# Inner norms of a two-layer diffusion step: two of eight chunks shifted and scaled by GpSimd

## The reference

```
def layer_norm(x, g, b):
    xf = x.astype(F32)
    xc = xf - xf.mean(-1, keepdims=True)
    var = (xc * xc).mean(-1, keepdims=True)
    return (xc * lax.rsqrt(var + EPS) * g + b).astype(x.dtype)

def modulate(x, shift, scale):
    return x * (1 + scale) + shift
...
for layer in range(DEPTH):
    hp = modulate(xp, mp[0], mp[1])            # the latent half (xs) likewise
    op = mixer(hp)
    xp = layer_norm(ALPHA * xp + mp[2] * op, ln_g[layer, 0], ln_b[layer, 0])
    hp = modulate(xp, mp[3], mp[4])
    fp = moe_ffn(hp, router_w, router_b, moe_wg[layer], moe_wu[layer], moe_wd[layer])
    xp = layer_norm(ALPHA * xp + mp[5] * fp, ln_g[layer, 1], ln_b[layer, 1])
```

## Time and profile before

| | |
|---|---|
| median of three runs | 1114.04 us (1110.41 to 1114.46) |
| the profiled execution's own time | 1112.55 us |
| its span in the trace | 1110.8 us |
| mean granted TensorE clock | 0.948 of full speed |
| busy: TensorE, VectorE, ScalarE, GpSimd | 983.9, 349.3, 217.0, 134.4 us |
| DMA | 299.5 MB, mean 270 GB/s |

### The profile page before, as it was taken

How to read it: one execution, slowest core, us unless ns; L and a number is a source line. 1 busy time by engine, 2 the same in 40 slices (tenths; PEclk the granted TensorE clock), 3 DMA queues, 4 the chain that set the end, 5 groups by cost and what they waited for, 6 DMA issues and landing times. The chain is left out here.

```text
span 1110.8 us, 13877 instructions
## 1 busy us (share of the span) xinstructions
PE 983.9 (89%) x5502; PEld 569.6 (51%) x5502; DVE 349.3 (31%) x820; ACT 217.0 (20%) x513; POOL 134.4 (12%) x149
## 2 busy tenths in 40 slices
PE   7899998897989898977999998899696989898986
PEld 3344466764323333336788677578585323333334
DVE  1101125248101010123333677668427400101004
ACT  2110045031200010013333421213102200000003
POOL 1000000000000000001000266575001000000000
PEclk9899999896989999998999899999896999999998
DMA  9995772162999999995655400222234699999981
GB/s 379 401 408 219 315 307 76 38 245 107 401 431 427 427 428 427 427 428 228 244 211 207 173 1 1 76 76 77 76 130 173 254 414 427 428 427 426 429 377 39
DMA packets 22444, 299.50 MB, mean 270 GB/s; under 512 B 2592, under 2 KB 2720, under 8 KB 4320
## 3 DMA queue, kind: packets, MB, share of 16 engines
q1 hardware_dynamic: 20880, 292.45, 64.3%
q0 software_dynamic: 1488, 6.03, 1.4%
HBM read 295.32 MB, written 3.15 MB: 269 GB/s over the span
## 5 line engine op out<-in xcount | busy, mean ns | idle before, releaser
L547 PE MATMUL bank<-ring,arena 128*32 128x512 f32 (+1 forms) x1216 | 203.0, 607 | 7.1 <-DMA ring<-slots 7.1
L565 PE MATMUL bank<-ring,arena 128*32 128x512 f32 (+1 forms) x608 | 112.4, 671 | 32.3 <-DMA ring<-slots 27.2
L547 PEld LDWEIGHTS bank<-ring,arena 128*32 128x32 f32 (+1 forms) x1216 | 61.2, 125 | 144.1 <-issue 133.6
L821 DVE TENSOR_TENSOR arena<-arena,bank 128x256 f32<-128x256 f32 x28 | 11.8, 421 | 302.1 <-ACT arena L650 302.1
L975 PE MATMUL bank<-act_t,ring 128*128 128x256 f32 x384 | 89.4, 387 | 6.3 <-DVE act_t L432 6.3
L1529 PE MATMUL bank<-ring,act_t 128*128 128x512 f32 x192 | 87.4, 608 | 3.2 <-DVE act_t L1794 2.5
L975 PEld LDWEIGHTS bank<-act_t,ring 128*128 128x128 f32 x384 | 72.4, 194 | 20.0 <-DVE act_t L432 6.7
L565 PEld LDWEIGHTS bank<-ring,arena 128*32 128x32 f32 (+1 forms) x608 | 32.1, 134 | 94.3 <-issue 84.5
L888 POOL COPY arena<-arena 128x512 f32 (+1 forms) x34 | 17.5, 515 | 391.8 <-PE bank L547 306.5
L1529 PEld LDWEIGHTS bank<-ring,act_t 128*128 128x128 f32 x192 | 36.3, 195 | 51.2 <-issue 46.4
L905 PE MATMUL bank<-act_t,ring 128*128 128x256 f32 x256 | 59.9, 396 | 1.6 <-ACT act_t L1267 0.9
(11 more groups left out here) (323 smaller groups left out, 1284.5 us busy)
## 6 DMA issues: line engine op xcount, KB each, us to landing
ring<-slots SPq DMA_DIRECT2D x138, 2048.0 KB, 12.7
cst<-consts SPq DMA_DIRECT2D x1, 1260.5 KB, 36.8
act_t<-x_t POOLq DMA_DIRECT2D x1, 1024.0 KB, 12.7
ring<-state POOLq DMA_DIRECT2D x1, 1024.0 KB, 5.2
out_st<-arena POOLq DMA_DIRECT2D x4, 256.0 KB, 2.8
out_y<-arena SPq DMA_DIRECT2D x4, 256.0 KB, 2.1
par<-params SPq DMA_DIRECT2D x1, 613.0 KB, 3.9
arena<-nat_bias POOLq DMA_DIRECT2D x1, 512.0 KB, 22.1
```

Of the source, the lines that this page charges most:

```text
L547: last = pe.matmul(bk[to:to + wide, :], x[:, 4 * m + c, wide * e:wide * e + wide], w[:, c, 512 * t:512 * t + 512], start=(m == 0 and c == ...
L565: last = pe.matmul(bank[3][to:to + wide, :], ht[:, col + wide * e:col + wide * e + wide], w[:, f, 512 * t:512 * t + 512], start=(f == 0), ...
```

## The change

In each inner norm chunks 7 and 3 go to GpSimd: for each chunk two instructions of 128 x 128 (one for each half of the tokens), a multiply and an add in one, with the two columns as scalars. It waits for the first L424 before chunk 7 and for the second before chunk 3, and raises `ln_h` once behind the fourth. ScalarE keeps chunks 4, 5 and 6, VectorE 0, 1 and 2. `ln_h` now counts three for a site, and the waits are changed to that, those of the last norm too.

```diff
--- before.py
+++ after.py
@@ -375,7 +375,7 @@
                 pe.wait_ge(S("ln_eps"), site + 1)
                 ada_rows(pe, jobs[k], bank[LN_JOB_BANKS[k]], jobs[0])
             if site < 3:
-                pe.wait_ge(S("ln_h"), 2 * site + 2)
+                pe.wait_ge(S("ln_h"), 3 * site + 3)
 
         def ln_act(act, ch, site):
             for h in range(4):
@@ -392,7 +392,7 @@
             if site < 3:
 
                 act.wait_ge(S("ln_norm"), 2 * site + 1)
-                for c in range(4, KC):
+                for c in range(4, 7):
                     for s in range(2):
                         i = site * 16 + 2 * c + s
                         last = act.activation(act_t[:, c, s * P:(s + 1) * P], res[:, c, s * P:(s + 1) * P], ACT.Identity,
@@ -426,18 +426,23 @@
             if site < 3:
 
                 dve.wait_ge(S("ln_norm"), 2 * site + 2)
-                rv = res[:, 0:4, :].rearrange("p c (s n) -> p (c s) n", s=2)
-                av = act_t[:, 0:4, :].rearrange("p c (s n) -> p (c s) n", s=2)
-                ch.link(dve.tensor_tensor(av, rv, bcast(mod_g[:, site * 16:site * 16 + 8], P), ALU.mult))
-                dve.tensor_tensor(av, av, bcast(mod_b[:, site * 16:site * 16 + 8], P), ALU.add).then_inc(S("ln_h"), 1)
+                rv = res[:, 0:3, :].rearrange("p c (s n) -> p (c s) n", s=2)
+                av = act_t[:, 0:3, :].rearrange("p c (s n) -> p (c s) n", s=2)
+                ch.link(dve.tensor_tensor(av, rv, bcast(mod_g[:, site * 16:site * 16 + 6], P), ALU.mult))
+                dve.tensor_tensor(av, av, bcast(mod_b[:, site * 16:site * 16 + 6], P), ALU.add).then_inc(S("ln_h"), 1)
             if site in LN_JOBS:
                 ada_store(dve, LN_JOBS[site][0], bank[LN_JOB_BANKS[0]])
 
         def ln_pool(pool, site):
 
-            pool.wait_ge(S("ln_norm"), 2 * site + 2)
-            if site < 3:
-                pool.wait_ge(S("ln_h"), 2 * site + 2)
+            for h, c in enumerate((7, 3)):
+                pool.wait_ge(S("ln_norm"), 2 * site + h + 1)
+                for s in range(2):
+                    i = site * 16 + 2 * c + s
+                    last = pool.tensor_scalar(act_t[:, c, s * P:(s + 1) * P], res[:, c, s * P:(s + 1) * P],
+                                              mod_g[:, i:i + 1], mod_b[:, i:i + 1], ALU.mult, ALU.add)
+            last.then_inc(S("ln_h"), 1)
+            pool.wait_ge(S("ln_h"), 3 * site + 3)
 
             for c in range(KC):
                 i = site * 16 + 2 * c
@@ -1666,7 +1671,7 @@
             for q in range(2):
                 for s in range(2):
                     for j in range(4):
-                        pe.wait_ge(S("ln_h"), 6 + 4 * q + j + 1)
+                        pe.wait_ge(S("ln_h"), 9 + 4 * q + j + 1)
                         last = pe.transpose(bank[2 * q + s + 2][:, j * P:(j + 1) * P], res[:, 4 * q + j, s * P:(s + 1) * P], ident)
                     last.then_inc(S("yt_done"), 1)
 
```

## The result

The changed kernel takes 1118.8 us as the median of 22 executions (1110.72 to 1127.24), the kernel before in the same comparison 1115.16 us (1108.15 to 1121.92, also 22). The ratio is 1.0039 with a 95% interval of 1.002 to 1.0058: slower, by about 0.4%; the interval reaches a little beyond 0.5%. Ratios here leave out two executions that count as slow (1126.37 us of the kernel before, 1122.01 us of best2), averages keep them. A ratio is an estimate of its own and need not be the quotient of the two medians. Forecast were "no change" by the mark of 0.5% and 1.25 us of loss, but also 1114.5 us with a range up to 1117.2, and the median lies 1.6 us above it. The profiled execution is the longest of this sample (1127.24 us, span 1125.4, granted clock 0.933); it is already 8.2 us behind at the first norm, where the two programs have been the same.

What follows compares the result with a forecast made beforehand. TensorE, busy 89% of the span, was taken as the bound. Three norms' 1.35 us loss less 0.1 us made 1.25 us on a base of 1113.3: forecast 1114.5 us, range 1110.9 to 1117.2.

Steps and rivals of the forecast that it cites:

- VectorE's pieces: Inner norms: the two broadcast instructions, cut to 768 elements, take 0.96 us alone, some 1.1 us with waiting for GpSimd.
- p: Inner norms: time of one 128x128 GpSimd instruction, taken as 0.44 us from the copies' slope, bounds 0.28 and 0.55.
- TensorE later by 0.44 us for each norm: Inner norms: GpSimd and VectorE take turns, GpSimd's fourth piece ends last, TensorE starts 0.44 us later; chance 0.68.
- The scaling of `res`: Behind each norm on GpSimd: ends 0.15 us earlier as seen from the router, 0.1 us in all in favour.
- A shift passes 1:1: Three inner norms: time won or lost there reaches the end of the run whole.
- no exclusion: Rival at the norms: GpSimd's pieces run beside VectorE, TensorE starts 0.53 us earlier each, 1111.7 us; chance 0.15.
- the base: Whole run: time of the kernel before, taken as 1113.3 us, midway between profiled execution and median of three runs.
- the sum: Whole run: 1.35 us lost at three norms less 0.1 us in favour, 1.25 us of loss.
- first three cases: Whole run: taking turns 1114.5 us (0.68), GpSimd beside VectorE 1111.7 (0.15), lower clock 1116.0 (0.11).
- A lower clock at site 0: Rival at the first norm's router: longer TensorE idle drops the clock, 1.45 us more, 1116.0 us; chance 0.11.
- theory C: Experiments' expectation: waits at norms also cost TensorE clock; filling them should cut the total by 2 to 5 us.
- taking turns for pointer-scalar pieces: Experiments' expectation: GpSimd and pointer-scalar VectorE instructions alternate, TensorE starting 4.5 to 4.8 us after the scaling starts.

Runs made afterwards that it cites:

- best2: Kernel before with the scaling in three parts, eight pieces on ScalarE, five pointer-scalar pieces on VectorE, three on GpSimd: ratio 0.9971, median 1110.98 against 1114.63 us.
- b_delay: Kernel before with two more VectorE passes ahead of its `ln_h` signal in each inner norm: ratio 1.0065, 7.7 +- 1.1 us slower.
- b_dummy: Kernel before, with GpSimd also computing chunks 7 and 3 into an unused place, so work is not divided: 1118.88 us, one execution.
- p3_only: Changed kernel with GpSimd taking chunk 3 alone, ScalarE keeping four chunks and VectorE three: ratio 0.9975 against the kernel before.
- b_ts: Kernel before, no GpSimd, VectorE's two broadcast instructions replaced by eight 128x128 ones with pointer scalars: ratio 0.9994.
- ts_split: Changed kernel with VectorE's three chunks done in six 128x128 pointer-scalar instructions: 1108.75 us, one execution.
- ts_timed: The changed kernel with six pointer-scalar VectorE instructions (ts_split) again, now with times: median 1110.16 against 1114.63 us, ratio 0.9994.
- best: Kernel before with no GpSimd in the inner norms, scaling in three parts, nine ScalarE pieces, seven pointer-scalar VectorE pieces: ratio 1.0003.
- b_again1: Kernel before, unchanged, profiled a second time, one execution: 1113.91 us.
- b_spin: Kernel before with extra constant matmuls (2, 11 and 6) filling TensorE's waits at the three inner norms: ratio 1.0001.
- a_spin: Changed kernel with the same extra constant matmuls in TensorE's waits as b_spin: ratio 1.0003 against b_spin.

## Why the prediction was wrong

**The mechanism at the norms was right, at each step.** VectorE's pieces: 1.1 us expected with their wait, 1.09 measured. GpSimd's piece: p = 0.44 us chosen, 0.446 measured. TensorE later by 0.44 us for each norm: 0.48. GpSimd last, ScalarE not: so. The scaling of `res` ends 0.12 us earlier as seen from the first router, 0.15 forecast. A shift passes 1:1: b_delay, 7.7 +- 1.1 us for 7.5. That GpSimd shuts out a VectorE instruction with two inputs in SBUF is shown by b_dummy, where the work is not divided, and by p3_only. The rival "no exclusion" fell with it for this kernel. The note on which I let it stand, that instructions in a two-port mode and GpSimd block each other (the Trainium skill, Advanced Engine Details and Errata, "VectorE Performance Modes"), does not say that only these do, and L431 took 1.35 us and not 1.22. The Trainium skill's GPSIMD Engine Reference, section "Specifications", names instructions with two SBUF inputs as well, and the trace agrees. For the size of a piece the slope of the copies was nearer (0.44 us) than the 0.36 that I had estimated from the best loop in the Trainium skill's GPSIMD Engine Reference, "Elementwise — side-by-side cycle accounting"; 0.446 was measured.

**The number was wrong by its base and its range, and by an excess of the effect that is mostly not explained.** In the comparison itself the kernel before has a median of 1115.16 us, 1.9 above the base of 1113.3, and the changed kernel lies 3.6 us above it, where the sum had 1.25. The step that failed first is the base. "I take the middle of the two as base, 1113.3" rested on three executions and one profile; 130 executions of the kernel before, over all sessions, average 1115.5 us. That is 2.2 of the 4.3 us between 1114.5 and 1118.8, and the spread it went by was that of three executions (4 us) where 22 show 14. The range did not even hold what the text says of it: half of the 4.1 us at either end of the first three cases (1111.7 to 1116.0) is 1109.7 to 1118.0, and 1110.9 to 1117.2 adds only 0.8 and 1.2. (The median would have missed the wider range too.) A good part of that spread is made ahead of the first norm: there the clock is 0.92 to 0.94 from 120 to 160 us in three of 17 profiles, and the first norm comes 5 us or more later.

The second is a term that the sum did not have, the clock behind the norms. It stood there only as a rival with a chance of 0.11 at site 0, and the second norm was not thought of. The profiles show something there, but neither its cause nor that it reaches the end:

| where | before, 3 profiles | changed, 4 profiles | difference of the averages |
|---|---|---|---|
| start of L424 to TensorE, three norms | 4.93 to 4.94 each | 5.41 to 5.42 each | 1.44 us |
| router to ScalarE's read, first norm | 2.23 in all | 2.23, 3.45, 2.24, 3.38 | 0.6 us |
| first 16 matmuls behind the second norm | 5.37, 5.81, 5.49 | 6.76, 6.55, 6.47, 6.52 | 1.0 us |
| router to ScalarE's read, third norm | 3.69, 3.42, 3.38 | 3.59, 3.31, 3.32, 3.30 | -0.1 us |

These add up to 2.9 us. "A lower clock at site 0" was there in two of four profiles of the changed kernel and in none of three before, at 1.2 us (I had priced it at 1.45). Idle time alone does not decide it: the two and the other two were idle for the same 2.12 us. At the third norm a shorter wait did go with a faster router. In the five runs in which TensorE was idle for 3.15 us or less (b_ts, ts_split, ts_timed, best, best2) the router took 1.07 us and ScalarE read its result 2.65 to 2.81 us behind its start; with 3.41 to 3.49 us idle it was 1.93 to 1.94 and 3.38 to 3.69 us. But with 3.75 to 3.97 us idle it was 1.33 to 1.84 and 3.08 to 3.59 us again. At the second norm the idle times do not order the durations, as said under b_again1.

Against the full 2.9 us speaks what is left of the run when the part ahead of the first norm is taken off. From the first L424 to the end of the span it is 868.8, 869.2 and 868.2 us in three profiles of the kernel before, and 875.1, 869.3, 868.6 and 869.4 in the four of the changed one. The first of these has the slow group of 10.05 us behind the second norm; the other three are 0.4 us above the kernel before on average, and not 2.9. Single profiles of the other runs lie up to 3 us off what their waits would give, so this settles no microsecond, but it does not show the clock's part in the end. Nor do b_spin and b_delay: in both a clock won or lost right behind a norm was not found in the total.

Four comparisons give 3.4 +- 1.25, 2.2 +- 1.5, -0.7 +- 1.2 and 3.2 +- 1.3 us, weighted by their errors 1.9 +- 0.6 us for the whole effect (they scatter somewhat more than their errors). The forecast of 1.25 is one error below that, and so not contradicted. So the loss at the waits is shown, 1.44 us, and its sum was right to 0.1; whether anything is added to it by the clock is open.

The third is chance. Taken over all sessions, of the 4.3 us 2.2 are the base and 0.65 the effect's excess over 1.25, and about 1.4 are left. The first comparison's 3.4 us lies above what four together give, and the changed kernel's 58 executions average 1117.8 and not 1118.9 us.

The forecast "within 0.5%" held for the ratio of each of the four comparisons, though three of the four intervals reach beyond. Of the expectations written for the experiments, theory C's gain from filled waits and my taking turns for pointer-scalar pieces fell.

## What to carry to other kernels

GpSimd as a third hand helps only beside VectorE instructions that do not shut it out: with a broadcast column as second SBUF operand the two engines work in turns, and with the same column as a pointer scalar, one instruction for multiply and add, they work side by side (5.42 against 4.24 us for the same division). It is the distance at the norms that this shortens; the totals do not show it yet. Look for a pair of overlapping instructions of the very form in the trace before dividing: a TENSOR_SCALAR with a constant did wait for GpSimd. And before a number is forecast from a kernel whose executions spread by 4 us, take a base from many executions, and look at how the profiles differ ahead of the change. A wait can be read from one profile to 0.01 us; the 58 executions of the changed kernel give its whole effect only to 0.6.

## What was not expected of the hardware

- Exclusion depends on the form of the VectorE instruction and not on SBUF as such. The pointer-scalar form at 128x128 took 0.27 us apart beside GpSimd as alone, but a TENSOR_SCALAR with a constant at 128x32 took up to 0.54 us in place of 0.18. Which of their differences does it is not shown. The pointer-scalar form is also the faster one alone: 2.14 us for what the broadcast pair did in 2.48.
- TensorE idle for the same 2.12 us, in four profiles of one program: the clock fell in two and stayed in two.
- A clock kept up by filling a wait fell all the same, some 7 us later, at the narrow matmuls of L984 (in b_spin, and likewise in a_spin); from the restart to the end of the next group it took 15.89 us in b_spin, and 15.84 in the kernel before.
- The part ahead of the first norm, the same in all programs here, had a granted clock of 1.00 from 120 to 160 us in 14 of 17 profiles and 0.92 to 0.94 in three, and came to the first norm at 238.7 to 243.0 us or at 247.9 to 250.3.
